# The narrow expert's halves: added by a shift product in place of the folds, with the activation by token row

## The reference, cut to what matters

```python
logits = (t @ w_router + b_router).astype(jnp.float32)
top_vals, top_idx = lax.top_k(logits, TOP_K)
top_w = jax.nn.softmax(top_vals, axis=-1)
combine = jnp.sum(jax.nn.one_hot(top_idx, N_EXPERTS) * top_w[..., None], axis=1)
for e in range(N_EXPERTS):
    out = out + combine[:, e:e+1] * swiglu(t, w_gate[e], w_up[e], w_down[e])
# swiglu(x, g, u, d) = (silu(x @ g) * (x @ u)) @ d
```

## Time and profile before

| | |
|---|---|
| median of 3 runs | 1425.57 us (1425.56 to 1428.21) |
| span of the profiled execution | 1420.5 us; its own time outside the span is not recorded, the median lies 5.1 us above the span |
| mean granted TensorE clock | 0.981 |
| busy: PE, DVE, ACT, POOL | 1352.7, 1249.7, 942.9, 140.5 us |
| transfers | 467.25 MB, mean 329 GB/s |
| the expert stage | about 530 to 1400 us |

### The profile page before, as it was taken

The page is one execution under the profiler, slowest core; times in us unless marked ns, Lnnn a source line. Parts: engine busy times, 40 slices in busy tenths (PEclk is TensorE's granted clock), DMA queues, the critical chain, the costliest instruction groups (busy, mean ns, idle before and its releaser), DMA issues.

```text
span 1420.5 us, 18379 instructions
## 1 busy us (share of the span) xinstructions
PE 1352.7 (95%) x7090; PEld 1136.9 (80%) x7090; DVE 1249.7 (88%) x1085; ACT 942.9 (66%) x885; POOL 140.5 (10%) x135
## 2 busy tenths in 40 slices
PE   3999799999999899999999999999999999999995
PEld 3868699998977688887788888888888888888884
DVE  6898898886858589999999999999999989999997
ACT  4465443333546468877786887887778887788783
POOL 4099200000058000000000000000000000000000
PEclk9999899999999999999999999999999999999998
DMA  8961799986562079999999999999999999999991
GB/s 327 382 248 49 281 325 330 337 303 216 191 223 90 1 281 397 396 396 400 400 394 393 399 399 396 396 401 388 388 396 397 399 403 390 380 398 401 396 402 72
DMA packets 189597, 467.25 MB, mean 329 GB/s; under 512 B 8734, under 2 KB 10940, under 8 KB 175164
## 3 DMA queue, kind: packets, MB, share of 16 engines
q1 hardware_dynamic: 189500, 465.98, 87.5%
HBM read 464.90 MB, written 1.05 MB: 328 GB/s over the span
## 4 chain that ended last, share of the span: by engine, by line
PE 83%; DVE 7%; DMA 6%; ACT 3%; issue 1%; SPq 0%; DVEq 0%; ACTq 0%
PE bank L1729 17%; PE bank L1730 16%; PE bank L1731 16%; PE bank L2196 6%; PE bank L2197 6%; PE bank L2239 3%; PE bank L2241 3%; PE bank L2215 3%; DMA raw<-in_w_ex_up 2%; DMA raw<-in_w_ex_down 2%; DVE w_lo L1397 1%; PE bank L2133 1%; PE bank L2142 1%; DMA raw<-in_w_ex_gate 1%; PE bank L1755 1%
## 5 line engine op out<-in xcount | busy, mean ns | idle before, releaser
L1397 DVE TENSOR_TENSOR w_lo<-raw,w_hi 128x2048 fp32r<-128x2048 f32 x202 | 455.8, 2286 | 32.7 <-ACT w_hi L666 32.0
L666 ACT ACTIVATE w_hi<-raw 128x2048 fp32r<-128x2048 f32 x202 | 382.2, 1917 | 55.5 <-DMA raw<-in_w_ex_up 20.3
L642 ACT ACTIVATE w_hi<-raw 128x2048 fp32r<-128x2048 f32 (+1 forms) x54 | 102.2, 1894 | 121.6 <-PE bank L1731 103.2
L1397 DVE TENSOR_TENSOR more_lo<-raw,more_hi 128x2048 fp32r<-128x2048 f32 x67 | 153.2, 2286 | 12.3 <-ACT more_hi L666 11.9
L1397 DVE TENSOR_TENSOR fifth_lo<-raw,fifth_hi 128x2048 fp32r<-128x2048 f32 x67 | 153.1, 2286 | 11.5 <-ACT fifth_hi L666 11.2
L1052 DVE TENSOR_TENSOR w_lo<-raw,w_hi 128x2048 fp32r<-128x2048 f32 (+1 forms) x54 | 123.6, 2294 | 24.5 <-ACT w_hi L642 24.3
L666 ACT ACTIVATE fifth_hi<-raw 128x2048 fp32r<-128x2048 f32 x67 | 128.4, 1916 | 21.6 <-DMA raw<-in_w_ex_gate 7.3
L666 ACT ACTIVATE more_hi<-raw 128x2048 fp32r<-128x2048 f32 x67 | 128.4, 1916 | 17.7 <-DMA raw<-in_w_ex_up 6.2
L1729 PE MATMUL bank<-h_hi,w_hi 128*128 128x256 f32 x448 | 128.3, 286 | 0.8 <-DVE gate_m L1111 0.8
L1730 PE MATMUL bank<-h_lo,w_hi 128*128 128x256 f32 x448 | 126.7, 283 | 0.0
L1731 PE MATMUL bank<-h_hi,w_lo 128*128 128x256 f32 x448 | 126.7, 283 | 0.0
(11 more groups left out here) (367 smaller groups left out, 2967.0 us busy)
## 6 DMA issues: line engine op xcount, KB each, us to landing
raw<-in_w_ex_gate SPq DMA_DIRECT2D x112, 1024.0 KB, 11.8
raw<-in_w_ex_up SPq DMA_DIRECT2D x112, 1024.0 KB, 12.0
raw<-in_w_ex_down SPq DMA_DIRECT2D x112, 1024.0 KB, 12.9
raw<-in_w_ada SPq DMA_DIRECT2D x48, 1024.0 KB, 7.0
raw<-in_w_in SPq DMA_DIRECT2D x12, 1024.0 KB, 8.9
raw<-in_w_ff_gate SPq DMA_DIRECT2D x10, 1024.0 KB, 6.6
raw<-in_w_ff_up SPq DMA_DIRECT2D x10, 1024.0 KB, 6.9
raw<-in_w_ff_down SPq DMA_DIRECT2D x10, 1024.0 KB, 5.8
```

Of the source, the lines that this page charges most:

```text
L642: act_e.activation(w_hi[:, s % SPLIT, 0:words], raw[:, n % RAW, 0:words], ACT.Copy).then_inc(hi_done, 1)
L666: act_e.activation(dst, raw[:, (N0 + n) % RAW, :], ACT.Copy).then_inc(hi_done, 1)
L1397: dve.tensor_tensor(lo, raw[:, (N0 + n) % RAW, :], hi.bitcast(F32), ALU.subtract).then_inc(lo_done, 1)
```

## The change

The halves are added where they lie, in PSUM, and the narrow activation takes the wide one's route. `keep_gate` and `keep_up` now write `g_low` and `u_low` in fp32r, without the reordering of columns. `add_s` runs one matmul a bank, `shift` (128x128, ones where row m + 64 meets column m, zero in columns 64 to 127) by the 512 columns of the copy, accumulating onto bank 2 and bank 3: the low tokens' half is added to partitions 0 to 63. ScalarE's SiLU reads bank 2 by token row into `f_tok` (128x512), VectorE multiplies by bank 3, and `turn_s` transposes `f_tok` in four 128x128 blocks into bank 2. ScalarE copies the high part of 64 columns of each block to `f_pack` (`high_s`), VectorE subtracts for the low part (`low_s`). `add_s` stands between the two units of the next chunk's wide gate, `turn_s` between the two of its wide up; for the last chunk of a pair they stand before and after the first unit of its wide down.

```diff
-            pool.memset(fold[:, :], 0.0).then_inc(pool_own, 1)
...
+            pool.tensor_copy(shift[:, 0:HALF], ident[:, HALF:P]).then_inc(shift_ready, 1)
+            pool.tensor_scalar(shift[:, HALF:P], ident[:, HALF:P], 0.0, None, ALU.mult).then_inc(shift_ready, 1)
...
+            def high_s(n):
+
+                act_e.wait_ge(f_tp, n)
+                act_e.activation(f_pack[:, :, 0:HALF], bank[2][:, :].rearrange("p (k t) -> p k t", t=P)[:, :, 0:HALF],
+                                 ACT.Copy).then_inc(fhi_done, 1)
...
-                    act_e.activation(in_blocks(g_pre[:, :]), by_row_pairs(bank[2][:, :]), ACT.Copy).then_inc(gate_kept, 1)
+                    act_e.activation(g_low[:, :], bank[2][:, :], ACT.Copy).then_inc(gate_kept, 1)
...
-                    act_e.wait_ge(folded, p * EC + (c + 1))
-                    act_e.activation(f_act[:, :, :], bank[2][:, 0:4 * HALF].rearrange("p (k t) -> p k t", t=HALF),
-                                     ACT.Silu).then_inc(fsilu, 1)
+                    act_e.wait_ge(s_added, p * EC + (c + 1))
+                    act_e.activation(in_blocks(f_tok[:, :]), by_row_pairs(bank[2][:, :]), ACT.Silu).then_inc(fsilu, 1)
...
+                    if u == ("L", "gate", 0, 0) and p > 0:
+                        high_s(p * EC)
+                        evacuate_l(p, 1)
+                    if u == ("S", "gate", c, 1) and c > 0:
+                        high_s(p * EC + c)
...
-                        if p + 1 < PAIRS:
-                            evacuate_l(p + 1, 1)
...
+            def low_s(n):
+
+                dve.wait_ge(fhi_done, n)
+                dve.tensor_tensor(f_pack[:, :, HALF:P], bank[2][:, :].rearrange("p (k t) -> p k t", t=P)[:, :, 0:HALF],
+                                  f_pack[:, :, 0:HALF].bitcast(F32), ALU.subtract).then_inc(flo_done, 1)
...
-                    dve.tensor_tensor(f_act[:, :, :], f_act[:, :, :],
-                                      bank[2][:, 4 * HALF:8 * HALF].rearrange("p (k t) -> p k t", t=HALF),
+                    dve.tensor_tensor(in_blocks(f_tok[:, :]), in_blocks(f_tok[:, :]), by_row_pairs(bank[3][:, :]),
                                       ALU.mult).then_inc(fact_done, 1)
-                    dve.wait_ge(fact_done, p * EC + (c + 1))
-                    h, l = f_pack[:, :, 0:HALF], f_pack[:, :, HALF:P]
-                    dve.tensor_copy(h, f_act[:, :, :]).then_inc(fhi_done, 1)
-                    dve.wait_ge(fhi_done, p * EC + (c + 1))
-                    dve.tensor_tensor(l, f_act[:, :, :], h.bitcast(F32), ALU.subtract).then_inc(flo_done, 1)
...
+                def add_s(c):
 
                     pe.wait_ge(gate_kept, p * EC + (c + 1))
                     pe.wait_ge(up_kept, p * EC + (c + 1))
-                    for i, pre in enumerate((g_pre, u_pre)):
-                        for a in range(4):
-                            o = (4 * i + a) * HALF
-                            last = mm(bank[2][:, o:o + HALF], pre[:, a * P:(a + 1) * P], fold[:, :], start=(i, a) == (0, 0),
-                                      stop=True, skip_group_check=True)
-                    last.then_inc(folded, 1)
+                    for b, low in ((2, g_low), (3, u_low)):
+                        last = mm(bank[b][:, :], shift[:, :], low[:, :], start=False, stop=True, skip_group_check=True)
+                    last.then_inc(s_added, 1)
+
+                def turn_s(c):
+
+                    pe.wait_ge(fact_done, p * EC + (c + 1))
+                    for a in range(4):
+                        last = pe.transpose(bank[2][:, a * P:(a + 1) * P], f_tok[:, a * P:(a + 1) * P], ident[:, :])
+                    last.then_inc(f_tp, 1)
...
-                    into_l("gate", c, 0)
+                    into_l("gate", c, 0, (0,))
+                    if c > 0:
+                        add_s(c - 1)
+                    into_l("gate", c, 0, (1,))
...
-                        fold_s(c - 1)
+                        pe.wait_ge(elo_done, p * EC + c)
+                    into_l("up", c, 1, (0,))
                     if c > 0:
-                        pe.wait_ge(elo_done, p * EC + c)
-                    into_l("up", c, 1)
+                        turn_s(c - 1)
+                    into_l("up", c, 1, (1,))
...
-                fold_s(LAST)
+                add_s(LAST)
+                down_l(LAST, (0,))
+                turn_s(LAST)
                 if p + 1 < PAIRS:
                     gather_l(p + 1, 1)
-                down_l(LAST)
+                down_l(LAST, (1,))
                 down_s(LAST)
```

More of the change, by code:

```diff
@@ L251, in trunk_kernel @@
         sel_ts = sb("sel_ts", [P, T], F32R, where=mixed)
-        now_s = sb("now_s", [P, 4], where=mixed)
-        w_slot = sb("w_slot", [P, 2], where=mixed)
+        f_tok = sb("f_tok", [P, 512], where=mixed)
         mixed.close()
@@ L272, in trunk_kernel @@
         chunked = sb("chunked", [P, T])
-        fold = sb("fold", [P, HALF])
+        shift = sb("shift", [P, P], F32R)
         slot_no = sb("slot_no", [P, P])
@@ L283, in trunk_kernel @@
         summed = ExitStack()
-        g_pre = sb("g_pre", [P, 512], where=summed)
-        u_pre = sb("u_pre", [P, 512], where=summed)
+        g_low = sb("g_low", [P, 512], F32R, where=summed)
+        u_low = sb("u_low", [P, 512], F32R, where=summed)
         summed.close()
@@ L336, in trunk_kernel @@
         e_lo = sb("e_lo", [P, 4, P], F32R, where=moe)
-        f_act = sb("f_act", [P, 4, HALF], where=moe)
         f_pack = sb("f_pack", [P, 4, P], F32R, where=moe)
@@ L358, in trunk_kernel @@
         now = sb("now", [P, 4], where=moe)
+        now_s = sb("now_s", [P, 4], where=moe)
+        w_slot = sb("w_slot", [P, 2], where=moe)
         w_before = sb("w_before", [P, G], where=moe)
@@ L598, in _ @@
                 pool.tensor_scalar(sin2[:, :, 0, half], trig[:, 0, :, :], -1.0 if i == 0 else 1.0, None, ALU.mult).then_inc(trig2, 1)
-            pool.memset(fold[:, :], 0.0).then_inc(pool_own, 1)
[L601 to L604, removed]
+            pool.wait_ge(consts, 1)
+            pool.tensor_copy(shift[:, 0:HALF], ident[:, HALF:P]).then_inc(shift_ready, 1)
+            pool.tensor_scalar(shift[:, HALF:P], ident[:, HALF:P], 0.0, None, ALU.mult).then_inc(shift_ready, 1)
             pool.wait_ge(cols_done, 2)
@@ L927, in keep_gate @@
                     used(("S", "gate", c, 1))
[L928 removed]
+                    act_e.activation(g_low[:, :], bank[2][:, :], ACT.Copy).then_inc(gate_kept, 1)
                 def keep_up(c):
                     used(("S", "up", c, 1))
[L932 removed]
+                    act_e.activation(u_low[:, :], bank[3][:, :], ACT.Copy).then_inc(up_kept, 1)
                 def silu_s(c):
[L935 to L937 removed]
+                    act_e.wait_ge(s_added, p * EC + (c + 1))
+                    act_e.activation(in_blocks(f_tok[:, :]), by_row_pairs(bank[2][:, :]), ACT.Silu).then_inc(fsilu, 1)
                 for j, u in enumerate(pair_order):
@@ L981, in _ @@
                 pair(p)
+            high_s(PAIRS * EC)
             act_e.wait_ge(split_used, S0 + E * NU)
@@ L1579, in pair @@
                         pair_lo_of(p, j)
+                    if u == ("L", "gate", 0, 0) and p > 0:
+                        low_s(p * EC)
+                        split_l(p, 1)
+                    if u == ("S", "gate", c, 1) and c > 0:
+                        low_s(p * EC + c)
                     if u == ("L", "up", 0, 0) and p > 0:
@@ L1627, in add_sum @@
                 dve.wait_ge(fin_acc, done + 2)
+            low_s(PAIRS * EC)
             dve.wait_ge(acc_done, 4 * (PAIRS - 1))
@@ L2176, in unit, with into_l @@
                     return f(pair_hi), f(pair_lo)
-                def into_l(kind, c, b):
-                    for half in range(2):
+                def into_l(kind, c, b, halves=range(2)):
+                    for half in halves:
                         wh, wl = unit(("L", kind, c, half))
@@ L2206, in turn_l, with down_l @@
                     last.then_inc(e_tp, 1)
-                def fold_s(c):
+                def add_s(c):
                     pe.wait_ge(gate_kept, p * EC + (c + 1))
                     pe.wait_ge(up_kept, p * EC + (c + 1))
-                    for i, pre in enumerate((g_pre, u_pre)):
-                        for a in range(4):
-                            o = (4 * i + a) * HALF
-                            last = mm(bank[2][:, o:o + HALF], pre[:, a * P:(a + 1) * P], fold[:, :], start=(i, a) == (0, 0),
-                                      stop=True, skip_group_check=True)
-                    last.then_inc(folded, 1)
-                def down_l(c):
-                    for pair_of in range(2):
+                    for b, low in ((2, g_low), (3, u_low)):
[6 more added lines that the diff above has]
+                    last.then_inc(f_tp, 1)
+                def down_l(c, parts=range(2)):
+                    for pair_of in parts:
                         pe.wait_ge(elo_done, p * EC + (c + 1))
@@ L2287, in _ @@
```

(2 more changed lines are left out.)

8 lines of the change are left out of this document (3 added, 5 removed).

## The result

The changed kernel takes **1451.47 us** (median of 4 runs, 1449.99 to 1453.30) against 1425.95 for the kernel before beside it: ratio 1.018, 95% interval 1.0164 to 1.0195. Slower, as forecast, but by 25.5 us and not by 10, and outside the range. The profiled execution has a span of 1450.9 us and took 1452.66, so 1.8 us lie outside the span. In nearly all timed runs of this case it is 1.7 to 1.9, in four of them up to 2.3. (The 5.1 us between the span and the median of before were thus mostly that its profiled execution was a quick one, about 1422.3 by this estimate.)

What follows compares the result with a forecast made beforehand. The weight stream, near 398 GB/s, was taken as the bound. Boundaries +7.3 us (3 x 3.7 - 3.8) and the end +2.65 made +9.95 on a 1420.5 us span, 1430.45, plus 5.1 outside it: 1435.5 us, range 1427.5 to 1443.5.

Steps and rivals of the forecast that it cites:

- the new stream loss per boundary: Weight stream lost behind each of three pair boundaries after the change: 3.7 us, within 2.7 to 6.1.
- 5.4 - 2.7: Lower bound of that loss: quickest landing 5.4 us after issue, less a remaining lead of 2.7, so 2.7 us.
- the present 1.6 plus all 4.5: Upper bound of the loss per boundary: the present loss plus the whole added lateness, 6.1 us.
- the lateness itself: At a boundary, how much later the pair ends against the arrivals of weights: 4.2 to 5.0 us.
- up to 0.8: How much later the last added halves of a pair lie against the arrivals, from waits in weight-paced chunks.
- My cover for the waits inside a pair: Inside a pair, where weights set the pace, a wait of 1.5 us or more before transposes costs nothing.
- Rival 2: Idle of 4 to 5 us at boundaries halves TensorE's clock, also at the end: +6.8 us, 1442.3; chance 0.17.
- The end: After the stage's last unit, product to first weighted row takes 7.95 us in place of 5.29: +2.65 us.
- Rival 1: At boundaries the stream does not mind, by queue slack or ScalarE catching up: 1426.4 or 1428.2; chance 0.16.
- 3 (the product not late): At the boundary VectorE finishes the last low parts sooner, so no wait: 1424.4 or 1421.8; chance 0.07.
- 4 (a dear shift product): In each chunk two shift products cost 1.84 us, 1.37 more: +29 us, 1454; chance 0.03.
- 28 x 0.82: TensorE work saved over all chunks by replacing folds with shift products and transposes: 23 us in all.

Runs made afterwards that it cites:

- late18: The kernel before, folds kept, with 18 useless matmuls (4.2 us) between wide and narrow down product at the three inner boundaries; 1435.79 us, ratio 1.0070.
- late36: The kernel before, folds kept, with 36 useless matmuls (8.4 us) between wide and narrow down product at the three inner boundaries; 1449.37 us, ratio 1.0173.
- busy: The changed kernel with useless matmuls in the idle, 18 before each pair's last transposes and 8 in the last chunk's wide up; 1440.17 us, ratio 1.0111.
- up_first: The changed kernel with the transposes inside a pair behind both wide up units, boundary unchanged; 1445.49 us, ratio 1.0143.
- early: The changed kernel with reordered pair boundaries and the last chunk's SiLU and gated product issued two units sooner; 1423.89 us, ratio 0.9996.
- down_first: The changed kernel with both wide down units ahead of the narrow transposes at a pair's end; 1433.31 us, ratio 1.0051.

## Why the prediction was wrong in size

What held, step by step. The direction and the mechanism held: the stream of weights is the bound, TensorE's savings inside a pair win nothing, and the boundary's late end goes into the stream. The shift products take 0.47 us for two, as worked out. The groups by shape of the changed kernel give the other prices:

```profile
L2231 PE MATMUL bank<-ident,f_tok 128*128 128x128 f32 x112 | 20.2, 308 | 37.3 <-DVE f_tok L1580 37.0
L1580 DVE TENSOR_TENSOR f_tok<-f_tok,bank 128x512 f32<-128x512 f32 x28 | 19.0, 679 | 0.0
...
L913 ACT ACTIVATE f_pack<-bank 128x256 fp32r<-128x256 f32 x28 | 10.4, 372 | 14.0 <-PE bank L2231 14.0
```

The product's 0.68 and the high part's 0.37 are those of the prediction. The idle before the last transposes, forecast 4 to 5 us, is 4.08. The other 14 waits share 37.0 - 16.3 = 20.7 us; they run from 0.16 to 2.21 us, 1.5 in the mean, the low edge of the 1.5 to 2.5 forecast. The product starts 7.72 us behind the added halves (1191.14 - 1183.42), where I took 7.56. Two slips in the working are small: 1174.59 to 1178.36 is 3.77 us and not 3.74, and 1182.5 lies 4.1 us behind 1178.36 and not 4.2.

**The step that failed first is the new stream loss per boundary, put at 3.7 us inside bounds of 2.7 and 6.1.** The profile has 8.6, outside both bounds. Over the 1.3 us that before loses in the mean it is 7.3 more, where 2.4 were reckoned. Two things are in it.

First, what a late us costs. I had both ends, "5.4 - 2.7" and "the present 1.6 plus all 4.5", and leaned to the low one because the page's typical landing time is that of a queue with several units in it. late18 and late36 say the upper end: 0.9 to 1.0 us per us. With that the forecast's own lateness gives 3 x 4.5 + 2.65 = 16 us, and busy, the change without its clock, measured 15.6.

Second, the lateness itself: "4.2 to 5.0". From added halves to weighted rows it is 18.86 - 12.95 = 5.9, and the extra is the clock, 3.60 us from the start of the transposes to the next unit (1191.87 to 1195.47) where 0.44 + 1.84 = 2.28 were reckoned, and some tenths around it. The place itself had moved by more than the "up to 0.8" that I allowed: the last chunk loses 1.99 us idle (at 1159.57) and half of the 3.4 us at clock 0.50 behind it (at 1160.7) while the shorter work gives 0.82 back, 2.9 us. 5.9 + 2.9 = 8.8 late, against 7.3 of stream lost. (The first pair is like this third one. The second has no half clock in its last chunk but a longer one about its transposes, and ends 1.2 + 6.9 = 8.1 late.) My cover for the waits inside a pair, "it costs nothing there, since a chunk is 31.6 us anyway", fails in the chunk before a boundary, where the pair's end is what counts; up_first puts these waits, with the half clock behind them, at 4.5 to 6.0 us.

**Rival 2, the clock, came true as well**, at every pair end, and not only there. I gave it 0.17, as an alternative to the forecast; it was an addition to it. Its price was 10 to 11 us (busy) and not 6.8: it also struck in the last chunk of three pairs (699.9, 1160.7 and 1392.8), which at the 1.7 us of the prediction is 5.1 more. The rule that I cited of the Trainium skill, "TensorE: Matmul & The Clock Gate", section "Why this matters for your kernels", would have had it at most boundaries, and the runs agree; what I held against it, that other work around the gap was thin in the one stretch of before, decided nothing. The sign that I named for this rival, a granted clock under 0.9 over chunks 1 and 2, would have missed it: it is 1.00, 0.98 and 0.97 there, since most of the half clock lies ahead of these stretches.

**The end**, "+2.65", is +6.2 (15.6 against 9.45). From the product's start to the weighted rows it is 10.3 us (1421.15 to 1431.42), with 7.95 reckoned. busy, at full clock, takes those 7.95 (1409.85 to 1417.80), so 2.3 are clock. The remaining 1.2 are that the product comes later behind the last high part: 5.35 us (1415.80 to 1421.15) against 4.16. That high part no longer waits for a transfer, so the engines, and not the transfers, set the pace there.

The sum then nearly closes in the profiles: 3 x 7.3 + 6.2 = 28.1 us, and from the stage's first narrow gate bank to its last weighted rows the changed kernel takes 902.9 us (528.5 to 1431.4) against 873.9, +29.0. The spans differ by 30.4 and the medians by 25.5. The profiled execution of before was a quick one, and that of the changed kernel, 1452.66, lay 1.2 above its median.

Rival 1 (slack in the queue), 3 (the product not late) and 4 (a dear shift product) are out: by late18, by the 4.08 us and by the 0.47.

**Where the expected gain went.** By the prediction's 28 x 0.82 the change takes 23 us of work off TensorE. early, in which no matmul waits for the product, is no faster than before. This fits the prediction: the stream was the bound, and before it lost only 3.8 us over all boundaries, of which early won 1.4 back.

## What to carry to other kernels

Where a stream of transfers runs with all its buffers in turn, count each us of a late release as one us, unless a run shows slack; here a median of 11.8 us from issue to landing looked like slack, and there was almost none. When instructions are moved so that a wait falls inside a busy engine's queue, look at what stands behind the wait, and put enough independent work in front of it: here one moved unit of 2.8 us was worth 17 to 18. And an idle that brings the clock down is paid twice, so a clock rival belongs into the sum of a forecast that has such an idle, not beside it.

## What the runs showed of the hardware

- The granted clock fell to 0.50 at all four idles of 4.08 us, with TensorE nearly full before them; in the second pair for 6.8 us. In the last chunk of three pairs it fell behind idles of 2.03, 1.99 and 1.92 us (698.98, 1159.57, 1391.37). It stayed at 1.00 behind five others of the same kernel that were as long: 2.00, 2.01, 2.21, 2.02 and 1.99 us (635.57, 667.35, 898.42, 930.03, 1359.84). So near 2 us the length of the idle alone does not decide; what does was not tested. Behind the 1.27 us of down_first it stayed at 1.00.
- Useless matmuls in an idle that can't be avoided were worth having: 26 of them a pair won 10 to 11 us.
- The stream of 1 MB loads ran at 397 to 398 GB/s late in a pair. With 4.2 and 8.4 us put in ahead of three pair ends, 12.6 and 25.2 us in all, the kernel took 11.2 and 24.8 us longer (late18, late36).
